# Last phase of a two-block kernel: 64 columns of every expert row move from the dense product to the gathered sum

## What is computed

```python
u = jnp.take(peer_u, i_blk, axis=0)
a = jax.nn.gelu(jnp.einsum("td,thkd->thk", x_blk, u)) * g_blk
v = jnp.take(peer_v, i_blk, axis=0)
return jnp.einsum("thk,thkd->td", a, v)
...
x = x + peer_ffn(h2, ...)
return rmsnorm(x, g_final)
```

## Time and profile before

| | us |
|---|---|
| median of 3 executions | 3050.6 |
| lowest and highest | 3049.17, 3053.84 |
| the profiled execution, its own time | 3057.47 |
| its span in the trace | 3055.7 |
| first slab's product starts at | 2578.8 |
| first squares of the result start at | 3039.5 |

### The profile page before, as it was taken

How to read it: one execution, slowest core, us unless ns; L and a number is a source line. 1 busy time by engine, 2 the same in 40 slices (tenths; PEclk the granted TensorE clock), 3 DMA queues, 4 the chain that set the end, 5 groups by cost and what they waited for, 6 DMA issues and landing times.

```text
span 3055.7 us, 36583 instructions
## 1 busy us (share of the span) xinstructions
PE 2632.4 (86%) x13061; PEld 2231.4 (73%) x13061; DVE 2171.4 (71%) x3234; ACT 1415.5 (46%) x2660; POOL 829.1 (27%) x563
## 2 busy tenths in 40 slices
PE   7999999999999999999999998887433007999997
PEld 6777878888888878889878898777433006888886
DVE  4997465454445565565455568999999987998888
ACT  4366454343434444545554443222299925332323
POOL 0000000010100000000000003766688864767553
PEclk9999999999999999999999999999755558999999
DMA  9543555655555556556435567999999996999997
GB/s 257 177 139 124 193 179 184 194 185 195 180 194 189 192 165 214 190 162 199 166 117 172 185 228 260 411 419 419 415 417 420 420 419 226 406 408 408 408 407 300
DMA packets 278133, 805.29 MB, mean 264 GB/s; under 512 B 33113, under 2 KB 73281, under 8 KB 243936
## 3 DMA queue, kind: packets, MB, share of 16 engines
q1 hardware_dynamic: 220400, 417.26, 40.6%
q0 software_dynamic: 57344, 385.91, 31.2%
q10 hardware_dynamic: 240, 0.18, 0.0%
HBM read 799.09 MB, written 4.19 MB: 263 GB/s over the span
## 4 chain that ended last, share of the span: by engine, by line
PE 32%; DMA 9%; POOL 9%; issue 6%; DVE 4%; ACT 1%; another core or an unknown queue 0%; DVEq 0%; ACTq 0%; POOLq 0%
POOL expert_rows L1981 8%; PE ps L215 6%; PE ps L217 6%; PE ps L216 6%; DMA expert_rows<-in_peer_u,index 5%; PE ps L2525 5%; DMA expert_pieces<-in_peer_v,piece_index 2%; DMA expert_pieces<-in_peer_v,const 1%; POOL expert_pieces L2364 1%; PE ps L2532 1%; PE ps L2534 1%; PE ps L2533 1%; DVE junk L2418 1%; PE ps L2067 1%; PE ps L2066 1%
## 5 line engine op out<-in xcount | busy, mean ns | idle before, releaser
L200 DVE TENSOR_TENSOR wl<-ring,wh 128x1024 fp32r<-128x1024 f32 (+2 forms) x616 | 732.1, 1230 | 620.6 <-ACT wh L195 619.0
L195 ACT CAST wh<-ring 128x1024 fp32r<-128x1024 f32 (+2 forms) x616 | 609.6, 1039 | 633.6 <-PE ps L217 576.7
L1981 POOL DMA_INDIRECT expert_rows<-in_peer_u,index x256 | 473.6, 1850 | 592.7 <-DVE wl L200 429.6
L215 PE MATMUL ps<-wh,th 128*128 128x512 f32 (+1 forms) x1472 | 580.5, 394 | 6.9 <-DVE wl L200 5.0
L217 PE MATMUL ps<-wh,tl 128*128 128x512 f32 (+1 forms) x1472 | 572.0, 389 | 0.0
L216 PE MATMUL ps<-wl,th 128*128 128x512 f32 (+1 forms) x1472 | 571.8, 388 | 0.0
L2418 DVE CUSTOM_DVE_ANT_0 junk<-expert_rows,h 128x2048 f32<-128x2048 f32 x217 | 494.1, 2292 | 38.6 <-DMA expert_rows<-in_peer_u,index 37.0
L215 PEld LDWEIGHTS ps<-wh,th 128*128 128x128 f32 x1472 | 277.7, 189 | 67.3 <-issue 6.4
L2457 DVE SCALAR_TENSOR_TENSOR x_and_pieces<-expert_pieces,const,x_and_pieces 128x896 f32<-128x896 f32 x256 | 291.2, 1149 | 39.7 <-DMA expert_pieces<-in_peer_v,piece_index 21.2
L217 PEld LDWEIGHTS ps<-wh,tl 128*128 128x128 f32 x1472 | 277.5, 189 | 57.3
L216 PEld LDWEIGHTS ps<-wl,th 128*128 128x128 f32 x1472 | 277.9, 189 | 55.1
(11 more groups left out here) (380 smaller groups left out, 4471.3 us busy)
## 6 DMA issues: line engine op xcount, KB each, us to landing
ring<-in_w_in SPq DMA_DIRECT2D x80, 1024.0 KB, 5.1
expert_slabs<-in_peer_v SPq DMA_DIRECT2D x128, 576.0 KB
ring<-in_w_up SPq DMA_DIRECT2D x64, 1024.0 KB, 5.3
ring<-in_w_down SPq DMA_DIRECT2D x64, 1024.0 KB, 5.1
ring<-in_w_in SPq DMA_DIRECT2D x68, 512.0 KB, 4.8
ring<-in_w_out SPq DMA_DIRECT2D x32, 1024.0 KB, 5.1
ring<-in_w_peer_q SPq DMA_DIRECT2D x16, 1024.0 KB, 5.2
ring<-in_w_ukv SPq DMA_DIRECT2D x8, 1024.0 KB, 5.5
```

The costliest lines, as they stand in the source:

```text
L195: self.nc.scalar.copy(self.wh[:, i % 2, two, 0:w], self.ring[:, i, two, 0:w]).then_inc(self.high_ready, 1)
L200: self.nc.vector.tensor_tensor(self.wl[:, i % 2, two, 0:w], self.ring[:, i, two, 0:w], self.wh[:, i % 2, two, 0:w].bitcast(F32), ALU.subtr ...
L215: mm(o, hi, wh, start=start and k == 0, stop=False)
L1981: nc.gpsimd.indirect_dma_start(p.rows[:, n % GR, :], None, peer_u, bass.IndirectOffsetOnAxis(ap=p.index[:, n:n + 1], axis=0)).then_inc(p.l ...
```

## The change

The border between gathered and dense columns moves from 896 to 960. The gathered pieces grow from 896 to 960 columns. The dense columns shrink from 1152 to 1088, and it is the plain products that lose these 64: the two parts of 320 columns become two of 288. The 512 columns in three passes stay. `summed` starts 1 KB lower, since it is larger. The number of DMAs, products, casts and adds stays the same, and only sizes change: a slab is 544 KB instead of 576, a piece 480 KB instead of 448, and the load and the store of the residual are cut at the new border.

```diff
-    PIECE, WHOLE, SPLIT = 896, 640, 512
+    PIECE, WHOLE, SPLIT = 960, 576, 512
     SUMMED = WHOLE + SPLIT
     PARTS = ((0, WHOLE // 2), (WHOLE // 2, WHOLE // 2), (WHOLE, SPLIT))
...
         slabs = place("expert_slabs", [P, SLOTS, SUMMED], at=-112 * KB)
-        summed = place("x_and_pieces", [P, NH, PIECE], at=-85 * KB)
+        summed = place("x_and_pieces", [P, NH, PIECE], at=-86 * KB)
         pieces = place("expert_pieces", [P, GR, PIECE], at=-78 * KB)
```

## The result

| | before, us | changed, us |
|---|---|---|
| median of 9 executions | 3051.19 | 3060.06 |
| lowest and highest | 3049.17, 3054.71 | 3057.74, 3062.16 |
| ratio, 95% interval | | 1.0024 (1.0016 to 1.0033) |
| profiled execution, span | 3057.47, 3055.7 | 3059.33, 3057.5 |
| slab 0 starts, squares start, between them | 2578.8, 3039.5, 460.7 | 2574.1, 3041.45, 467.3 |

The changed kernel is slower, by 7.3 us by the ratio (4.9 to 10.1) and by 8.9 by the medians. The profiled executions show only 1.9 us, because that of before has a stall that its typical execution seems to lack: it lies 6.3 us above its own median. This row of its timeline, from the spreading of the weights ahead of slab 0, shows 5 us in which DVE waited for something outside the records; ACT stood for 4.6 us beside it.

What follows compares the result with a forecast made beforehand. The prediction took DMA, full from 2600 us on at about 407 GB/s, to bound the last phase. Bytes +8.4 and the end -4.5 gave +3.9 us on the 3050.6 us median: 3054.5 us, range 3044 to 3062.

Steps and rivals of the forecast that it cites:

- rival 1: Last phase: end backlog stays or waits leave DMA gaps; first form +8.1 to +8.8 us, some 3059; with gaps 3063; chance 0.25.
- the likeliest: Last phase: DMA-bound with the end's time given back, 3054.5 us, own range 3052.5 to 3057; chance 0.56.
- DMA is the ceiling, PE's relief finds no idle moment: Last phase: DMA is full from 2600 us on, so PE's saved 27.5 us meet no idle transfer time; 3.63 us a slab.
- The bytes: +8.4 us: Full DMA stretch of the last phase: 3.57 MB more pass, costing 8.4 us, taken between 8.1 and 8.8.
- price by bytes: Full DMA stretch: the 3.57 MB more, priced at 407.5 GB/s, cost 8.8 us.
- packet price: Full DMA stretch: the added bytes priced by packet time, 0.0372 ns a byte from comparing q0 with q1, cost 8.1 us.
- DVE has cover: Adds of pieces: 124 ns more a slab, DVE occupied 3.31 us, 91% of DMA's 3.63 us a slab.
- rival 4: Slab and piece transfers: sizes off multiples of 512 bytes cost the next multiple, 33.9 us less 4.5, 3080 us; chance 0.04.
- The end: -4.5 us: Last byte to the squares: 3.5 us in place of 8.5, 5.0 given back, between 0 and 6.0, taken as 4.5.
- "slower": Whole kernel: time above 3056.7 us, beyond the 0.2% band; chance 0.29.
- "same": Whole kernel: within 0.2%, 3044.5 to 3056.7 us; chance 0.60.

Runs made afterwards that it cites:

- transfers alone: Changed kernel's pieces of 960 and slabs of 1088 columns, but plain products 320 and adds 896 wide as in the kernel before: 1.0026 against the kernel before.
- PE alone: Kernel before with only PE's plain products cut from 320 to 288 columns in slabs 1 to 127: 0.9992 against the kernel before.
- late adds: 10 of 256 adds left until after the last slab's low parts; against the kernel before: changed kernel 1.0024, kernel before 1.0010, border at 912 1.0012.

## Why the prediction came out as it did

The range held (3054.5 forecast, 3044 to 3062; measured 3060.06), and the argument that decides, bytes against PE's relief, was right. But the sum was half of what came, +3.9 against +7.3 us, and the case is rival 1 in its first form rather than the likeliest: bytes set the time, and the end gave back almost nothing. That rival had 0.25 and the likeliest case 0.56; the range held because it was wide enough to take in both.

- *DMA is the ceiling, PE's relief finds no idle moment.* Right: transfers alone 1.0026, PE alone 0.9992. The distance between slabs was 3.63 us as computed, and 3.75 on the other side of the border.
- *The bytes: +8.4 us.* Right as far as the runs can tell. Both shares scale with bytes (25.3 and 24.6 bytes a ns at either size), which speaks for the price by bytes, +8.8; the packet price of 8.1 took a fixed part from comparing q0 with q1, which another row size does not show. But from slab 0 to the end of DMA's full work the two profiles give 452.2 and 459.4 us, only 7.2 apart, and the times with and without the gathers' 64 columns differ by 17.9 or 20 us where the two prices say 18.2 and 17: single profiles and these intervals do not choose between 8.1 and 8.8.
- *DVE has cover.* Right: 1217 ns against 1215, and the run without the longer adds is not faster. *Sizes off a multiple of 512 bytes* (rival 4): refuted: the rate stays 408 GB/s with rows of 3840 and 4352 bytes. This also agrees with the 256-byte unit of the Trainium skill, "DMA: Bandwidth & Descriptors", section "How a descriptor splits into AXI transactions".
- *The end: -4.5 us.* This step failed. The squares start 7.9 us behind the last byte as the prediction counts it (3033.5 to 3041.45) where it had been 8.5, so 0.6 came back; from the last gather's issue it is 12.2 us where it had been 13.2. I had the newest slab land last, then 2.5 us of casts and products and 1 us for the signal of the landing, and nothing queued behind it. No row shows that 1 us, and the end did not hang on it: the cast of the last slab waited for PE, not for a landing. The timeline of the changed kernel shows what stands there:

```profile
3029.22 1.04 POOL L2364 DMA_INDIRECT expert_pieces<-in_peer_v,piece_index  x1 [0.76 <-DVE x_and_pieces L2457]
...
3030.03 2.34 DVE L2457 SCALAR_TENSOR_TENSOR x_and_pieces<-expert_pieces,const,x_and_pieces 128x960 f32<-128x960 f32 x2
...
3033.47 2.34 DVE L2457 SCALAR_TENSOR_TENSOR x_and_pieces<-expert_pieces,const,x_and_pieces 128x960 f32<-128x960 f32 x2
...
3036.90 2.34 DVE L2457 SCALAR_TENSOR_TENSOR x_and_pieces<-expert_pieces,const,x_and_pieces 128x960 f32<-128x960 f32 x2
...
3040.31 2.35 DVE L2457 SCALAR_TENSOR_TENSOR x_and_pieces<-expert_pieces,const,x_and_pieces 128x960 f32<-128x960 f32 x2
```

The last gather can only be issued once as many adds are left as there are slots, 8. These 8 adds are bound, two at a time, to the low parts of the last 4 slabs, 3.43 us a group, so from the last issue to the last add there are 13.4 us, and DMA, no longer fed, delivers its full work in 4. DVE works off the rest without a pause, and PE's last three-pass products start when DVE has made the last low part (3040.4), three groups behind. The runs with 6 slots move this distance with the ring, in both kernels. In the kernel before, the chain of waits at the end is PE's alone, 3.54 us a slab; in the changed kernel it would be 3.32 by PE, but DVE's group holds it at 3.43, and the change itself made that group longer (3.22 us before). So the last slabs follow each other only 0.1 us faster than before. That a shorter ring or another order would give the 4.5 us back is not shown: neither made the kernel faster.

With the measured sizes the sum is +8.8 - 0.6 = +8.2 us; the ratio says 7.3 (4.9 to 10.1), the last phase of the two profiles 6.6. The chance given to "slower", 0.29, and to "same", 0.60, lay on the two sides of a line at 0.2% that the result, 0.24%, barely crosses.

Open: what the rare stall of 2 to 5 us in the spreading is, and why POOL's issue follows DVE's adds as it does (last section). The residual and the gain (2.2 MB through the full stretch) were not tried elsewhere.

## What to carry to other kernels

When two ways of doing the same work share out between engines and DMA, write down the pace of each resource per step (here PE 3.54, DMA 3.56, DVE 3.19 us) and move the border only towards the one with room; at the crossing point a step either way loses, 0.24% for 64 columns towards DMA and 0.67% towards PE. Judge whether DMA is the ceiling by a rate that stays flat where the engines' load varies, not by a share near 1. For the end of a phase count how many steps of the consumer lie behind the last issue that the slot ring allows, and price each of them at the engine that makes it: work that is moved behind the last step is paid there in full.

## What the runs showed of the hardware

- The DMA share reads 0.97 to 1.01 at 361, 385 and 391 GB/s as well as 1.02 at 408: a packet is on record for longer there (q0 at 361 GB/s: 93.06 MB / (6720 x 0.588) = 23.6 bytes a ns, against 25.3; with the border at 832, where q0 moved 88.86 MB at 53.5% from 2600 to 3020 us, 24.7), and the share counts that as busy.
- A gather's issue on POOL took 0.94 to 1.04 us at the end of the changed kernel, where DVE's adds stand singly, and 1.95 us where DVE added without a pause. There POOL kept step with DVE: in the three kernels with late adds (960, 896 and 912 columns) an issue took 1.95, 1.82 and 1.86 us and a gather was issued every 2.25, 2.13 and 2.16 us, twice the distance between two adds (1.13, 1.06 and 1.08 us). With the adds at equal distances, each issue ended 0.8 us behind the end of the add in whose course it started. What ties the two together no run here isolates.
- One profile can hold a stall that the median lacks: 5.0 us in that of before, 3.6 us and less in two others, at the same place in the program.
